# Fifteen weight splits moved from GpSimd to VectorE in a decoder layer

## What is computed

```python
u = rms_norm(h, norm_mix[l])
z = u @ w_in[l]
y_rwkv = rwkv7_time_mix(z[..., :RWKV_IN], ...)            # 8 heads x 64, a scan over time
q, k, v = jnp.split(z[..., RWKV_IN:], 3, axis=-1)
y_moba = moba_attention(q, k, v)                          # 8 heads x 64, causal
h = h + jnp.concatenate([y_rwkv, y_moba], axis=-1) @ w_mix_out[l]
h = h + memory_cross_attention(rms_norm(h, norm_xattn[l]), rms_norm(mem, norm_mem[l]),
                               w_xq[l], w_xkv[l], w_xo[l])
a = jnp.square(jax.nn.relu(rms_norm(h, norm_ffn[l]) @ w_ff1[l]))
h = h + a @ w_ff2[l]
```

## Time and profile before

| | |
|---|---|
| time, median of three runs | 587.88 us (585.97 to 588.59) |
| span of the profiled execution | 586.1 us |
| TensorE busy | 539.1 us, 92% |
| VectorE busy | 355.8 us, 61%, 510 instructions |
| ScalarE busy | 260.1 us, 44% |
| GpSimd busy | 81.2 us, 14%, 72 instructions |
| low parts made by VectorE, GpSimd | 115, 15 |

### The profile page before, as it was taken

How to read it: one execution, slowest core, us unless ns; L and a number is a source line. 1 busy time by engine, 2 the same in 40 slices (tenths; PEclk the granted TensorE clock), 3 DMA queues, 4 the chain that set the end, 5 groups by cost and what they waited for, 6 DMA issues and landing times.

```text
span 586.1 us, 10849 instructions
## 1 busy us (share of the span) xinstructions
PE 539.1 (92%) x4594; PEld 511.7 (87%) x4594; DVE 355.8 (61%) x510; ACT 260.1 (44%) x394; POOL 81.2 (14%) x72
## 2 busy tenths in 40 slices
PE   3979779999889999998899998989999999999994
PEld 3966778989877888896898997989999999999994
DVE  4674997373444654543668663876766766766753
ACT  3858442423224443213335443547464463654622
POOL 8322330031101101112052000430000000000000
PEclk9998999999979999988999999989999999999998
DMA  8742243021402202222263521545656565645402
GB/s 272 251 143 74 73 144 111 33 81 65 144 1 73 73 1 74 74 73 92 73 197 107 199 86 60 160 148 173 208 175 191 170 203 164 209 156 205 144 1 73
DMA packets 61764, 72.57 MB, mean 124 GB/s; under 512 B 1282, under 2 KB 52564, under 8 KB 61716
## 3 DMA queue, kind: packets, MB, share of 16 engines
q1 hardware_dynamic: 61636, 71.61, 38.4%
q0 software_dynamic: 80, 0.26, 0.2%
HBM read 70.82 MB, written 1.05 MB: 123 GB/s over the span
## 4 chain that ended last, share of the span: by engine, by line
PE 72%; DVE 9%; ACT 2%; issue 2%; POOL 1%; DVEq 0%; ACTq 0%; POOLq 0%
PE bank L631 15%; PE bank L633 15%; PE bank L632 15%; PE bank L806 7%; PE bank L609 2%; DVE w_lo L1285 2%; PE bank L610 2%; PE bank L611 2%; DVE X L1499 1%; PE bank L990 1%; PE bank L742 1%; PE bank L958 1%; ACT w_hi L1022 1%; PE bank L954 1%; PE bank L918 1%
## 5 line engine op out<-in xcount | busy, mean ns | idle before, releaser
L631 PE MATMUL bank<-op_hi,w_hi 128*128 128x256 f32 x944 | 274.2, 290 | 7.2 <-DVE w_lo L1285 6.5
L632 PE MATMUL bank<-op_lo,w_hi 128*128 128x256 f32 x944 | 268.7, 285 | 0.0
L633 PE MATMUL bank<-op_hi,w_lo 128*128 128x256 f32 x944 | 268.6, 285 | 0.0
L1022 ACT ACTIVATE w_hi<-raw 128x1024 fp32r<-128x1024 f32 x130 | 137.2, 1058 | 145.5 <-PE bank L633 124.0
L631 PEld LDWEIGHTS bank<-op_hi,w_hi 128*128 128x128 f32 x944 | 182.8, 194 | 11.9 <-issue 10.2
L1285 DVE TENSOR_TENSOR w_lo<-raw,w_hi 128x1024 fp32r<-128x1024 f32 x115 | 144.6, 1258 | 65.3 <-ACT w_hi L1022 64.8
L632 PEld LDWEIGHTS bank<-op_lo,w_hi 128*128 128x128 f32 x944 | 182.9, 194 | 0.2
L633 PEld LDWEIGHTS bank<-op_hi,w_lo 128*128 128x128 f32 x944 | 182.7, 193 | 0.0
L533 POOL TENSOR_TENSOR w_lo<-raw,w_hi 128x1024 fp32r<-128x1024 f32 x15 | 37.1, 2470 | 200.6 <-ACT w_hi L1022 200.6
L806 PE MATMUL bank<-neu 128*128 128x128 f32 x320 | 42.2, 285 | 5.1 <-DVE neu L1509 4.2
L806 PEld LDWEIGHTS bank<-neu 128*128 128x128 f32 x320 | 39.2, 198 | 7.5 <-DVE neu L1509 5.3
(11 more groups left out here) (223 smaller groups left out, 568.6 us busy)
## 6 DMA issues: line engine op xcount, KB each, us to landing
raw<-in_w_ff SPq DMA_DIRECT2D x32, 1024.0 KB, 5.4
raw<-in_w_in SPq DMA_DIRECT2D x13, 1024.0 KB, 5.3
raw<-in_w_xkv SPq DMA_DIRECT2D x8, 1024.0 KB, 5.5
raw<-in_w_mix_out SPq DMA_DIRECT2D x4, 1024.0 KB, 5.2
raw<-in_w_xq SPq DMA_DIRECT2D x4, 1024.0 KB, 5.1
raw<-in_w_xo SPq DMA_DIRECT2D x4, 1024.0 KB, 5.3
xval<-in_x SPq DMA_DIRECT2D x2, 512.0 KB, 4.5
xkey<-in_mem SPq DMA_DIRECT2D x1, 1024.0 KB, 7.8
```

The lines of the kernel that those rows point to most:

```text
L631: mm(dst, wh[:, k, c:c + 128], op_hi[which][:, xk, :], start=first, stop=False)
L632: mm(dst, wh[:, k, c:c + 128], op_lo[which][:, xk, :], start=False, stop=False)
L633: last = mm(dst, wl[:, k, c:c + 128], op_hi[which][:, xk, :], start=False, stop=final)
L1022: op(view(w_hi), r, ACT.Copy).then_inc(hi_done, 1)
```

## The change

The list of splits for GpSimd is emptied. VectorE makes all 130 low parts, each at its own quarter. GpSimd keeps its constants, the product for `AR`, the tails and the squares. Since the list is empty, TensorE and SyncE wait only for VectorE's counter of low parts.

```diff
-POOL_SPLITS = [*range(3, 12, 2), *range(21, 2 * OUTS[FIRST["mix"]][0], 2)]
+POOL_SPLITS = []
```

## The result

The changed kernel is faster: 583.96 us against 588.59 us, a ratio of 0.9917 with a 95% interval of 0.9896 to 0.9938 (4.9 us, 3.7 to 6.1). The span of the profiled execution is 582.4 us, 3.7 us under that of before.

What follows compares the result with a forecast made beforehand. TensorE, busy 92% of the span, was taken as the bound, so moved work costs only where it waits for VectorE. Terms -2.3 - 0.5 + 0.6 + 0.8 + 0.2 = -1.2 us gave 586.7 us, range 584.6 to 589.8.

Steps and rivals of the forecast that it cites:

- the three that were named: VectorE delays beside GpSimd's low parts: subtraction at 36.07 us, two products at 58.14, addition at 127.93; 2.04, 1.89, 1.78 us lost.
- The two waits in line: VectorE's sum for U near 152 us and group 3's addition and masks near 196 us stand behind moved low parts: +0.6, +0.8 us.
- splits 3 to 11: Five early low parts, 21 to about 60 us: VectorE's delays go and TensorE's gaps shrink, -2.3 us, between -0.6 and -2.5.
- split 23: Low part right before VectorE's addition at 127.93 us: 1.78 us of delay go, 1.23 are added, -0.5 us.
- 27: A value head's low part near 152.6 us: the sum for U stands behind it and TensorE waits, +0.6 us.
- 31: Low part at 195.56 us, before the addition at 195.43 and the masks at 196.53: TensorE waits for the masks, +0.8 us.
- 39: Low part at 268.35 us, before the centring at 269.38: +0.2 us, bounds 0 and 1.2.
- the other six: Low parts 21, 25, 29, 33, 35 and 37: hidden while VectorE waits for TensorE, nothing; 1.2 us each without that cover.
- rival (d): TensorE's clock: half the 158 to 190 us loss regained, 584.9 us, 11%; or a low stretch after 74.05 us, 588.5, 10%.
- (a): Long VectorE durations are not GpSimd's doing, so 5.7 us of delays stay: 592.4 us, slower; 4%.
- (b): Waiting in line costs the full 1.23 us at splits 23, 25, 27, 31 and 39: +6.1 there, 591.7 us; 9%.
- (c): Early gain only in the first gap, VectorE being full from 61 to 87 us: -0.6 for -2.3, 588.4 us; 12%.

Runs made afterwards that it cites:

- the ten later splits: Kernel before with only the low parts of odd splits 21 to 39 moved from GpSimd to VectorE: ratio 0.9978 to before, taken again 0.9995.
- the kernel that reads idle data: Changed kernel plus five unused 128x1024 subtractions on GpSimd at the moments of splits 3, 5, 7, 9 and 11: ratio 1.0021 to before.

## Why the prediction was wrong

*What was right.* GpSimd's low parts held VectorE up, and these delays went: the three that were named, to the form's usual time each. The two waits in line came where they were placed. The steps, read matmul for matmul, came within half a microsecond of the forecast: -2.8 us for splits 3 to 11 (forecast -2.3; the difference may be the lower level that ends at 45 in place of 48 us), -0.76 for split 23 (forecast -0.5), +0.7 for 27 (forecast +0.6), +0.8 for 31 (forecast +0.8), +0.1 for 39 (forecast +0.2), nothing for the other six. Together -2.0 us against -1.2; at the low stretch near 160 us the changed kernel loses 0.25 us, which leaves -1.7.

*What was wrong.* The step that failed is the clock's term in the sum, which stood at zero, and rival (d), which was to cover it. I took the clock as it was in the one profile of before and let the work behind 87 us shift through it unchanged. I gave the clock a chance only at 158 to 190 us and before 74 us, and the 158 to 190 stretch was not regained: both profiles after have it, from 158 or 159 us on. What came on top lay behind the last moved split: a stretch near 386 us in all three profiles of before, worth 1.2 us, and one near 277 us in one of them, worth 3.2, neither of which is in the profiles after. The mean clock is 0.970 before (134 executions), 0.9775 after (25), and a fit over all kernels of time against kernel and mean clock leaves -2.7 +- 0.6 us (two standard errors) to the change at equal clock. The mean differs by 4.6 us. So by the fit about 2 us are the clock; the steps of the traces, which give the places 1.7 to 2.0 us, would leave nearly 3 to it. The forecast had it at zero. The fit is rough, as the mean clock doesn't say what a stretch costs; for the ten later splits it leaves 0.0 us, where the traces say +1.1. The shares are an estimate; that both exist is shown.

*The rivals.* (a) fell at the timeline and at the kernel that reads idle data. (b) was right in kind at 27 and 31 and cost 1.5 us there, not 6.1 over five places, and its price counted a full 1.23 us at split 23 although the 1.78 us of delay there would go in any case. (c) fell: from 61 to 87 us nothing is given back. The size of the range was wrong for a reason that the three times of before didn't show (585.97 to 588.59 us): over more executions the same kernel runs from 584.3 to 592.7 us. The mean clock goes with under a third of that spread (correlation -0.54 over the 134 executions; those at 0.975 and above average 586.4 us, those at 0.967 and below 589.6). The start varies by 2 us too; what makes up the rest is open.

*Open.* Why the stretches near 277 and 386 us come in one kernel and not in the other is not settled. The runs show that 0.7 us of work added near 207 us can turn it in both directions, and that it needn't touch the work near the stretches. They don't show a rule by which one could say beforehand which kernel gets one: 1.0 to 1.2 us of delay on VectorE didn't raise the clock.

## What to carry to other kernels

An idle engine isn't free help: before giving GpSimd an elementwise instruction, look for VectorE instructions with SBUF operands beside it, and price them at their own time plus what GpSimd has still to run. Look for it in a trace as a long VectorE row that ends with a GpSimd row. Where TensorE is near its limit and a change moves work by a microsecond, read the granted clock of several executions of both kernels before the difference is put down to the edit, and leave a range of some 3 us to either side for it (one stretch cost 3.2 us here).

## What was not expected of the hardware

Behind the same gap of 1.85 us near 386 us TensorE runs at 0.91 of the clock or at 1.00 (means of 380 to 400 us), and with 0.7 us of matmuls added near 207 us it changed from one to the other, in both directions. An added VectorE sum of 1.2 us cost 3.4 us on VectorE's chain, since it pushed GpSimd's read onto the next instruction. Three memsets on GpSimd, 3 us long, cost a two-operand VectorE instruction beside them nothing (1.22 us).
